# Moving the split of the RWKV output weights into the key projections, and the norm's shift to GpSimd

## What is computed

```python
def rwkv_out(y, h, xx, r, k_mod, v, mu, ln_g, ln_b, r_k, g1, g2, wo):
    bsz, n, d = r.shape                                  # 512 tokens, 1024 channels, 16 heads of 64
    y = layernorm(y, ln_g.reshape(RWKV_HEADS, RWKV_HEAD), ln_b.reshape(RWKV_HEADS, RWKV_HEAD), GN_EPS)
    bonus = jnp.einsum('bthk,zbthk->bth', _heads(r) * r_k, _heads(k_mod))
    y = y.astype(r.dtype) + bonus[..., None] * _heads(v)
    xg = h + xx * mu[5]
    gate = jax.nn.sigmoid(xg @ g1) @ g2
    return (y.reshape(bsz, n, d) * gate) @ wo
```

## Time and profile before

| | us |
|---|---|
| median of 3 runs | 4103.84 |
| lowest and highest | 4101.23, 4109.36 |
| span of the profiled execution | 4112.8 |
| projections, start to start of the gates | 192 |
| gates | 105 |
| scan | 650 |
| last stage | 122 |

### The profile page before, as it was taken

One profiled execution on the slowest core, in us unless ns is written; L12 is line 12 of the kernel. 1 busy time (PEld: TensorE's weight loads), 2 busy tenths in 40 slices (PEclk: granted clock), 3 DMA queues, 4 the chain that ended last, 5 costly groups with the idle time before them and its releaser, 6 DMA issues. The chain is left out here.

```text
span 4112.8 us, 81477 instructions
## 1 busy us (share of the span) xinstructions
PE 3751.5 (91%) x32632; PEld 2698.0 (66%) x32632; DVE 2406.6 (59%) x3924; ACT 1216.2 (30%) x2692; POOL 1320.8 (32%) x1020
## 2 busy tenths in 40 slices
PE   8889999898999999998999997987899999899887
PEld 6667878657787898775344446755888888643332
DVE  4568873536884455564444447736888886623333
ACT  3352223343222322331111113233454544211111
POOL 4444443434445364661000001413454543000000
PEclk9999999999999999999999999998999998899999
DMA  4115542303553222347999991544232324399997
GB/s 127 54 52 184 184 154 72 102 1 140 177 184 124 90 63 75 113 139 314 420 420 420 420 420 55 193 170 137 55 81 59 78 67 151 129 403 422 421 421 310
DMA packets 228789, 781.62 MB, mean 190 GB/s; under 512 B 55512, under 2 KB 63529, under 8 KB 168721
## 3 DMA queue, kind: packets, MB, share of 16 engines
q1 hardware_dynamic: 222592, 757.93, 49.5%
q0 software_dynamic: 5328, 19.40, 1.2%
q10 hardware_dynamic: 576, 0.09, 0.0%
HBM read 730.06 MB, written 47.28 MB: 189 GB/s over the span
## 5 line engine op out<-in xcount | busy, mean ns | idle before, releaser
L3951 PE MATMUL scan_bank<-scan_T,scan_off 64*64 64x64 f32 x3840 | 167.1, 225 | 44.1 <-issue 31.5
L3011 ACT ACT_TABLE_LOAD x32 | 41.1, 1283 | 519.6 <-PE moe1e_p_u L2957 262.8
L2887 POOL DMA_INDIRECT moe0e_xg<-moe_h,moe_first_rows x20 | 18.9, 947 | 546.2 <-DVE moe_first_rows L3044 540.5
L3951 PEld LDWEIGHTS scan_bank<-scan_T,scan_off 64*64 64x64 f32 x3840 | 143.6, 140 | 53.2 <-issue 37.2
L373 POOL TENSOR_TENSOR gmi_w_lo<-gmi_rows_w,gmi_w_hi 128x512 fp32r<-128x512 f32 x64 | 120.2, 1878 | 159.6 <-ACT gmi_w_hi L415 159.6
L373 POOL TENSOR_TENSOR p_w_lo<-p_rows_w,p_w_hi 128x512 fp32r<-128x512 f32 (+3 forms) x88 | 113.2, 1288 | 161.5 <-ACT p_w_hi L415 161.5
L2887 POOL DMA_INDIRECT moe1e_xg<-moe_h,moe_first_rows x17 | 16.0, 940 | 449.0 <-DVE moe_first_rows L3044 443.3
L1227 DVE SCALAR_TENSOR_TENSOR f0u_ada<-hT,condition,f0u_ada 128x512 f32<-128x512 f32 x168 | 152.2, 974 | 13.4 <-DMA hT<-in_ada_w_dram 12.9
L1159 POOL TENSOR_TENSOR f1u_w_lo<-f1u_w,f1u_w_hi 128x1024 fp32r<-128x1024 f32 x42 | 114.5, 2745 | 138.4 <-ACT f1u_w_hi L1175 138.4
L1159 POOL TENSOR_TENSOR f0u_w_lo<-f0u_w,f0u_w_hi 128x1024 fp32r<-128x1024 f32 x42 | 114.6, 2750 | 137.7 <-ACT f0u_w_hi L1175 137.7
L1227 DVE SCALAR_TENSOR_TENSOR f1u_ada<-hT,condition,f1u_ada 128x512 f32<-128x512 f32 x168 | 141.0, 907 | 20.6 <-DMA hT<-in_ada_w_dram 20.1
(11 more groups left out here) (883 smaller groups left out, 11610.0 us busy)
## 6 DMA issues: line engine op xcount, KB each, us to landing
moe_ring<-in_moe_w_down_dram SPq DMA_DIRECT2D x140, 1024.0 KB, 18.2
gm_uT<-in_moe_w_gu_dram SPq DMA_DIRECT2D x111, 1024.0 KB, 16.6
moe_ring<-in_moe_w_gu_dram SPq DMA_DIRECT2D x102, 1024.0 KB
walk_memory<-in_moe_w_gu_dram SPq DMA_DIRECT2D x61, 1024.0 KB, 24.4
hT<-in_ada_w_dram SPq DMA_DIRECT2D x48, 1024.0 KB, 6.8
f0u_w<-in_ffn_w_gate_up_dram SPq DMA_DIRECT2D x22, 1024.0 KB, 4.8
f1u_w<-in_ffn_w_gate_up_dram SPq DMA_DIRECT2D x22, 1024.0 KB, 4.8
gmi_rows_w<-in_ga_w_in_dram SPq DMA_DIRECT2D x64, 256.0 KB, 2.7
```

Of the source, the lines that this page charges most:

```text
L2887: pool.indirect_dma_start(xg[:], None, H.h, bass.IndirectOffsetOnAxis(rows[:, 0:1], 0)).then_inc(gathered, 16)
L3011: nc.scalar.activation(sg[:], p_g[:], ACT.Silu).then_inc(silu_ready, 1)
L3951: mm = nc.tensor.matmul(out[r], lhsT[r], rhs[r], start=start, stop=stop, skip_group_check=True)
```

## The change

The split of `wo` leaves the scan. A new class hooks into the projections: at every third of the 48 steps (steps 0, 3, ... 45) one block is loaded, rounded by ScalarE behind that step's `w_hi`, subtracted by GpSimd behind that step's `w_lo`, and both halves are stored. There is one buffer each for the raw block and its halves; SyncE stores block i and loads block i+1 in its turn for step 3i+5. SyncE waits for all stores at the stage's end. The addition of the shift leaves the scan too: the last stage loads the whole shift, its first load, into the buffer that later holds another row, GpSimd adds it to the four tiles of bonus rows (128 x 1024 each) ahead of its routing rows, and VectorE waits for the tile before it adds the bonus rows. The row that reuses the buffer is loaded behind a wait for all four adds. The values of a later head are loaded behind a wait for the bonus that read the buffer.

```diff
 (project_split, SyncE)
                     if fetch:
                         fetch.load(sp, t)
+                    if other:
+                        other.move(sp, t)
 
                     if c and k == KT - 1 and jobs[c - 1].get("stores"):
                         store(c - 1)
+                if other:
+                    other.store(sp, other.blocks - 1)
+                    sp.wait_ge(other.halves_stored, 32 * other.blocks)
 (project_split, GpSimd, behind w_lo of step t)
+                    if other:
+                        other.low(pool, t)
 (project_split, ScalarE, behind w_hi of step t)
+                    if other:
+                        other.high(act, t)
 (rwkv_scan, SyncE)
-                    sp.wait_ge(s["lo_made"], h + 1)
-                    for d, w in zip(wo, (w_hi, w_lo)):
-                        sp.dma_start(block_of(d, h), w[:].bitcast(F32)).then_inc(s["w_stored"], 16)
-                    if ahead is not None:
-                        sp.wait_ge(s["bonus_shifted"], h + 1)
-                        load_raw(ahead)
                     if walk is not None:
                         sp.wait_ge(s["y_copied"], walk + 1)
                         if ahead is not None:
+                            sp.wait_ge(s["bonus_done"], walk + 1)
                             load_v(ahead)
 (rwkv_scan, ScalarE)
                     walk_both(1)
-                    act.wait_ge(s["raw_loaded"], 32 * h + 32)
-                    act.wait_ge(s["w_stored"], 32 * h)
-                    A(w_hi[:], w_raw[:], ACT.Copy).then_inc(s["hi_made"], 1)
                     copy_turned(0)
 (rwkv_scan, VectorE)
                     add_bonus()
-                    split_block()
-                    add_shift()
 (walk_finish, SyncE)
+                sp.dma_start(shift[:], a["rw_ln_b_2"].partition_broadcast(P)).then_inc(shift_loaded, 16)
                 sp.dma_start(gain[:], a["rw_ln_g_2"].partition_broadcast(P)).then_inc(consts_loaded, 16)
...
                 R.fetch_rows(sp)
+                sp.wait_ge(shifted, NT)
                 sp.dma_start(row[:], mods[0, 2 * D:3 * D].partition_broadcast(P)).then_inc(row_loaded, 16)
 (walk_finish, GpSimd)
+                pool.wait_ge(shift_loaded, 16)
+                for t in range(NT):
+                    nc.gpsimd.tensor_tensor(bonus[:, t, :], bonus[:, t, :], shift[:], ALU.add).then_inc(shifted, 1)
                 R.make(pool, 0)
 (walk_finish, VectorE, join of tile t; the same ahead of the last head's join)
+                    dve.wait_ge(shifted, t + 1)
                     c.step(V.tensor_tensor(y[:, t, early], y[:, t, early], bonus[:, t, early], ALU.add))
+class OutputSplit:
+    EVERY = 3
...
+    def at(self, t):
+        return t // self.EVERY if t % self.EVERY == 0 and t // self.EVERY < self.blocks else None
+    def load(self, sp, i):
+        sp.dma_start(self.raw[:], self.block(self.w, i)).then_inc(self.raw_loaded, 16)
+    def store(self, sp, i):
+        sp.wait_ge(self.lo_made, i + 1)
+        for dst, x in zip(self.parts, (self.hi, self.lo)):
+            sp.dma_start(self.block(dst, i), x[:].bitcast(F32)).then_inc(self.halves_stored, 16)
+    def move(self, sp, t):
+        if t == 0:
+            self.load(sp, 0)
+        i = self.at(t - 5) if t >= 5 else None
+        if i is not None and i + 1 < self.blocks:
+            self.store(sp, i)
+            self.load(sp, i + 1)
+    def high(self, act, t):
+        i = self.at(t)
+        if i is not None:
+            act.wait_ge(self.raw_loaded, 16 * i + 16)
+            if i:
+                act.wait_ge(self.halves_stored, 32 * i)
+            self.nc.scalar.activation(self.hi[:], self.raw[:], ACT.Copy).then_inc(self.hi_made, 1)
+    def low(self, pool, t):
+        i = self.at(t)
+        if i is not None:
+            pool.wait_ge(self.hi_made, i + 1)
+            if i:
+                pool.wait_ge(self.halves_stored, 32 * i)
+            self.nc.gpsimd.tensor_tensor(self.lo[:], self.raw[:], self.hi[:], ALU.subtract).then_inc(self.lo_made, 1)
```

More of the change, by code:

```diff
@@ L255, in load, with project_split @@
             sp.dma_start(dst[:], src).then_inc(done, 16)
-def project_split(nc, name, S, idle, hT, n_tok, jobs, parts=None, aside=None, fetch=None, shift=None, ring=4, ahead=None, stored=None):
+def project_split(nc, name, S, idle, hT, n_tok, jobs, parts=None, aside=None, fetch=None, shift=None, ring=4, ahead=None, stored=None, other=None):
     RAW = len(ahead.tiles) if ahead else ring
@@ L271, in project_split @@
         loaded = ahead.sems if ahead else [st.sem(f"loaded{b}") for b in range(RAW)]
+        st.sems += other.sems if other else []
         w_hi_made, w_lo_made, x_hi_made, x_lo_made = (st.sem(n) for n in ("w_hi_made", "w_lo_made", "x_hi_made", "x_lo_made"))
@@ L3514, in load_decays, with rwkv_scan @@
         self.load(sp, h, self.decays, "sg_loaded")
-def rwkv_scan(nc, name, S, a, kF, rF, sgF, aF, vS, y, bonus_rows, wo, last, ahead_of):
+def rwkv_scan(nc, name, S, a, kF, rF, sgF, aF, vS, y, bonus_rows, last, ahead_of):
     NG = STEPS // 4
@@ L3557, in rwkv_scan @@
         Sm, X, SA = last.Sm, last.X, last.SA
-        w_raw, w_hi, w_lo = sb("w_raw", [P, BANK]), sb("w_hi", [P, BANK], F32R), sb("w_lo", [P, BANK], F32R)
-        shift = sb("shift", [P, HK])
         bon = sb("bonus", [P, NT])
@@ L3571, in rwkv_scan @@
                  "off_ready z_ready z_copied zr_ready zr_added eed_made "
[L3572 to L3573 removed]
+                 "bon_ready bon_read bonus_done km_made kh_made factor_step tables_loaded bon_half").split()
         s = {n: st.sem(n) for n in names} | last.sems | ahead_of.sems
@@ L3909, in add_bonus @@
                         last.then_inc(s["bonus_done"], 1)
[L3911 to L3914, removed]
-                                        ALU.add).then_inc(s["bonus_shifted"], 1)
-                    def split_block():
-                        dve.wait_ge(s["hi_made"], h + 1)
-                        V.tensor_tensor(w_lo[:], w_raw[:], w_hi[:], ALU.subtract).then_inc(s["lo_made"], 1)
                     add_bonus()
-                    split_block()
-                    add_shift()
                     if ahead is not None:
@@ L4190, in walk_finish @@
         gain, row = st.sb("gain", [P, D]), st.sb("row", [P, D])
+        shift = row
         g = [st.sb(f"gate{u}", [P, EARLY]) for u in range(2)]
@@ L4606, in _, with __init__, block @@
                 add_bias(3)
+class OutputSplit:
+    EVERY = 3
+    def __init__(self, nc, mem, w, parts):
+        self.nc, self.w, self.parts = nc, w, parts
+        self.blocks = KD * 2
+        self.raw = mem.enter_context(nc.sbuf_tensor("wo_raw", [P, BANK], F32))
+        self.hi, self.lo = (mem.enter_context(nc.sbuf_tensor(f"wo_{n}", [P, BANK], F32R)) for n in ("hi", "lo"))
+        self.raw_loaded, self.hi_made, self.lo_made, self.halves_stored = (nc.alloc_semaphore(f"wo_{n}") for n in ("raw_loaded", "hi_made", "lo_made", "halves_stored"))
+        self.sems = [self.raw_loaded, self.hi_made, self.lo_made, self.halves_stored]
+    def block(self, w, i):
+        return w[i // 2 * P:(i // 2 + 1) * P, i % 2 * BANK:(i % 2 + 1) * BANK]
+    def at(self, t):
[27 more added lines that the diff above has]
+            self.nc.gpsimd.tensor_tensor(self.lo[:], self.raw[:], self.hi[:], ALU.subtract).then_inc(self.lo_made, 1)
 class GateWeights:
@@ L4861, in rwkv @@
                                  epi=copy_to(lambda j, n0, q=q: by_token[q][:, j, :]), stores=v_stores(q), mix=None if q else mixed(3)))
-            project_split(nc, "rp", S, 0, mix, ALL, jobs, shift=shift, fetch=gate_weights, ahead=S.rp_rows, stored=stored)
+            project_split(nc, "rp", S, 0, mix, ALL, jobs, shift=shift, fetch=gate_weights, ahead=S.rp_rows, stored=stored, other=out_split)
             S.rp_memory.close()
@@ L4871, in rwkv @@
     y, bonus = (mem.enter_context(nc.sbuf_tensor(f"rw_{n}", [P, NT, D], F32)) for n in ("y", "bonus"))
-    rwkv_scan(nc, "scan", S, a, kF, rF, sgF, aF, vS, y, bonus, wo, walk, first_head)
+    rwkv_scan(nc, "scan", S, a, kF, rF, sgF, aF, vS, y, bonus, walk, first_head)
     head_memory.close()
```

10 lines of the change are left out of this document (3 added, 7 removed).

## The result

The changed kernel takes 4116.06 us (median of 12 runs, 4106.01 to 4121.54), the kernel before in the same session 4106.86 us (12 runs, 4101.23 to 4111.76): ratio 1.0022, 95% interval 1.0014 to 1.0029. It is 9.2 us slower, where +3.0 was forecast; the time lies inside the range, near its upper end, and on the side that had 0.24.

What follows compares the result with a forecast made beforehand. No single bound in either stage: VectorE paces the middle of a head, TensorE's stream its front. Scan -2.7, projections +4.1, queues +1.0, last stage +0.6 gave +3.0 us on the 4103.84 median: 4106.8 us, range 4094 to 4117.

Steps and rivals of the forecast that it cites:

- the side that had 0.24: Whole kernel: the outcome slower than before, given chance 0.24, against 0.60 for same and 0.16 for faster.
- The scan: Scan: freed VectorE time counts only where a head's first add or next scan operation starts earlier; -2.7 us.
- shorter by over 10 us: Scan: a shrinkage this large would refute the scan term's second step; 2 to 4 us was expected.
- Rival 1: Scan: the freed VectorE time counts in full, -24 us with the other terms, 4080 us; chance 0.16.
- The port block: Projections: GpSimd's added subtractions lengthen VectorE operations with two SBUF inputs, 4.5 hits at 0.91 us; +4.1 us.
- Block 0: First key job: the block falls before VectorE's only free stretch there, the slow first products; 0 us.
- Its version of the sum: Projections: under a strict exclusive lock, each blocked operation pays GpSimd's whole operation, 1.26 instead of 0.91 us; 1.6 us higher.
- The late raw block: Read jobs of the projections: one output-weight block arrives late and TensorE waits; +1.0 us, bounds 0 and 11.4.
- rival 2: Read jobs: six blocks land late, ScalarE stands with the next w_hi behind; 11.4 us instead of 1.0, 4117.2 us; chance 0.24.
- a landing past 3.8 us costs: Read jobs: each us a raw block lands later than 3.8 us after issue costs TensorE one us.
- three issues of about 0.35: Read jobs: SyncE issues two stores and the next block's load at about 0.35 us each, 3.3 us after step start.
- The last stage: Last stage: GpSimd's third and fourth shift adds block two VectorE join operations, delaying TensorE's transposes; +0.6 us, bounds 0 and 2.7.

Runs made afterwards that it cites:

- scan_small_ops: Kernel before, with VectorE's split cut to 8 of 512 columns from head 1 on and its shift to one of four tiles, all transfers kept; scan 636.9 us.
- scan_no_moves: Kernel before, with VectorE's and ScalarE's operations whole but the loads and stores of split and shift only for heads 0 and 1; scan 643.6 us.
- two_raw: Changed kernel with two buffers for the raw block, so a block is loaded three steps earlier; projections' stage 193.4 us.
- two_all_small: Changed kernel with two buffers for raw block and each half, GpSimd's subtraction of blocks 2 to 15 on 8 of 512 columns; projections' stage 190.0 us.

## Why the prediction was off by 6 us, and where it held

**The scan: mechanism right, size too small.** Head 0 was to give 1.9 us: its first add came 1.90 us earlier after its bonus, and the head gave 2.69. Head 1 was to give 0.19, since lw comes next, and its scan operation does start 0.19 us sooner in its head. Yet plain heads shrank by 0.4 to 0.6 us (39.49 and 39.70 to 39.07 to 39.10), head 13 among them, which was to give nothing (39.7 to 39.1). The step that failed: the gain of a head was read from the starts of its first add and scan operation alone, with "heads nearly as long as before"; that VectorE's operations behind them keep their lengths was taken for granted. They do so only as long as they meet GpSimd's at the same places. With VectorE 0.19 us earlier and GpSimd's mask 0.65, the scan operation took 0.56 instead of 0.95 us. That makes 0.59 us (0.19 and the 0.40 between 0.88 and 0.48 above), and at the head's end it is 0.78 (39.83 to 39.05 us, the second execution of each; 0.45 in the first). With that the scan's term is -6.4 us (643.1 to 636.7), not -2.7. The sign "shorter by over 10 us" shows in the first pair of profiles (12.4), not in the second (6.3). Rival 1, which counts the freed time in full, stays out: 30.7 us of VectorE bought 6. That VectorE's time is what bought it, scan_small_ops and scan_no_moves show; that the rest of it comes from the changed meeting with GpSimd is read from head 1's rows, and was not tried by itself.

**The port block: mechanism right, size too small.** Forecast 4.5 hits at 0.91, +4.1; measured +7.9 (two of all buffers): 5.7 us of waits for x_lo (2.0 inside the stage before, 7.7 with two of all buffers), 1.6 of TensorE's clock (0.53 behind the wait at step 18 here too, see the last section), and 0.6 not assigned. The step that failed is the count of hits: one block hits more than one operation. 0.91 was read off a single hit, and hits at step 18 cost about that, 0.94. But there the added operation met x_hi and pushed GpSimd's next w_lo onto x_lo, so one block brought two. The largest new or longer waits came at steps 4, 6, 18 and 22 of the changed kernel, where 4, 7, 19 and 22 were named. Block 0 was put at 0, but costs 1.07 us ahead of the 7.9: x_hi of the first step ran under it and x_lo under the next w_lo, and TensorE's first wait, which ends where the stage lengths of the table begin, grew from 7.82 to 8.89 us. Little decides this: with two of all buffers, where x_hi began 0.01 us before GpSimd's operation and not 0.04 behind it, that wait stayed at 7.81. The Trainium skill ("SBUF — State Buffer", section "SBUF: two separate sides") has the engine that comes second block for the whole instruction of the first. The ends in the rows of step 18 agree with that, and so does a cast that began 0.55 us before GpSimd's operation ended and grew by 0.39 only (0.82 us, at 2629.60 in the changed kernel). Its version of the sum, 1.6 us higher, was nearer by luck: it raised the price of a hit, where the number of hits was too small.

**The late raw block: rival 2's mechanism, at part of its price.** Forecast 1.0, measured 4.1. The threshold (a landing past 3.8 us costs) did not hold as stated: blocks that took 4.05 and 4.7 us from issue to ScalarE's copy brought TensorE no wait for w_lo, one of 4.75 us brought 0.63; the median was 4.5, the longest 6.3. What failed above all was "three issues of about 0.35": beside a bulk store each took 1.1 to 1.3 us, so the load left 2 us late before its landing was late too. ScalarE stood before six blocks, TensorE felt two. ScalarE's waits for the raw block of more than 1 us are what the prediction named as the sign of rival 2.

**The last stage:** 0.6 foreseen, 0.45 measured to the transposes; the fourth add took a join operation to 3.12 us as the row of before did. The stage as a whole is 122.0 to 122.2 us after 120.3 to 121.9.

**Sum.** +7.9 + 1.1 (block 0) + 4.1 - 6.4 + 0.5 = +7.2 us from profiles, +9.2 (interval 5.7 to 11.9) in the runs. The rest isn't assigned; one execution's scan scatters by more than that (649.0 and 643.1 for the same kernel). That the time lies inside the range is in part luck: the terms of the projections were 8 us too small and the scan's 3.7 too small the other way, so the errors partly cancel. The profile that the prediction worked from was the long one: heads 1 to 14 took 563.9 us there and 558.9 in the second, most of the difference being TensorE's stalls at the front of heads.

## What to carry to other kernels

Work given to GpSimd is not free beside a VectorE that sets the pace: put it at steps at which VectorE has room, not at even distances (16 blocks every third step cost 12 us, the same 16 elsewhere, with more buffers, 0.9). A background transfer that an engine in the main chain waits for needs a buffer more than its landing time suggests, for the load and for the store, as some of the queue's issues themselves grew beside bulk stores (1.1 to 1.3 us instead of 0.35 to 0.5). And before a gain or loss of 0.2% is read from stages, profile the old kernel twice.

## What the runs showed of the hardware that was not expected

A wait can cost more than its length. Behind the 3.08 us wait at step 18, the granted clock of the changed kernel by stretch (columns as in the earlier trace rows):

```profile
2598.40:2602.00 3.60, 3.58 (x9) 2.83 (x10) 2.32 (x4) 0.00 (x0) 0.00 (x0) 0.53 0.87 239
2602.00:2605.60 3.60, 3.60 (x18) 2.87 (x17) 2.46 (x3) 0.63 (x1) 1.60 (x1) 1.00 1.02 399
```

At a clock of 0.53, near the lower of the two levels (1.2 GHz), TensorE made 9 matmuls in 3.6 us, then 18 in the same time at full clock: the wait of 3.08 us cost some 1.6 us more (8 intervals of 0.43 instead of 0.23 us). Behind the 4.05 us wait the interval was 0.43 us again, for as many matmuls. Behind the 1.20 us wait of before the clock stayed full. The length of the wait alone does not decide: behind one of 2.60 us in two_raw TensorE made 16 matmuls in 3.6 us at a clock of 1.00, behind one of 2.38 us in two_all_small 9 at 0.55. What else decides, these runs don't show. The Trainium skill ("TensorE: Matmul & The Clock Gate", section "HAM oscillation — how this bites in real kernels") describes waits for data after which the next work starts at half rate; the rows behind 3.08 and 4.05 us agree, here with waits for VectorE and GpSimd. This is why the stage grew by more than the waits for x_lo that the block caused.

A cast with one SBUF input (0.43 us) grew to 1.37 us under a GpSimd operation, just as the operations with two inputs did; the prediction had counted only those, though before has such a cast too (1.54 us instead of 0.56, at 2535.21).
